# The end of a mixture-of-experts layer: last weight copy on GpSimd, late matmuls inside both branches, merges behind the late loads

## What is computed

```python
# xn: RMS-normalised x, 1024 x 1024; 64 experts of width 256, top 8 per token, plus one shared expert
def swiglu(x, w_gate, w_up, w_down):
    return (silu(x @ w_gate) * (x @ w_up)) @ w_down
routed = sum over the 8 experts e of a token: weight[token, e] * swiglu(xn[token], w_eg[e], w_eu[e], w_ed[e])
out = x1 + routed + swiglu(xn, w_sg, w_su, w_sd)        # x1: x after the output projection
```

## Time and profile before

| | us |
|---|---|
| median of 3 runs | 1374.88 (1374.83 to 1376.29) |
| profiled execution, its own time | 1375.44 |
| span of that execution, first to last instruction | 1373.7 |
| last job's down product starts and ends on PE | 1331.67, 1335.33 |
| six loads and three merges issued from | 1341.84 and 1342.37 |
| last add on DVE ends | 1371.32 |

### The profile page before, as it was taken

The page is one execution under the profiler, slowest core; times in us unless marked ns, Lnnn a source line. Parts: engine busy times, 40 slices in busy tenths (PEclk is TensorE's granted clock), DMA queues, the critical chain, the costliest instruction groups (busy, mean ns, idle before and its releaser), DMA issues.

```text
span 1373.7 us, 23742 instructions
## 1 busy us (share of the span) xinstructions
PE 1346.1 (98%) x5711; PEld 552.6 (40%) x5712; DVE 991.1 (72%) x2364; ACT 695.3 (51%) x654; POOL 563.2 (41%) x713
## 2 busy tenths in 40 slices
PE   7999999999999989999999999999999999999998
PEld 3445455555555433333333333333333333333333
DVE  2656655656544468888888888888888888888852
ACT  1223334243244214666666666666666666666640
POOL 3010313313121553555555555555555555555531
PEclk9999999999999999999999999999999999999999
DMA  9522212112029437999999999889999999999927
GB/s 341 213 76 85 62 54 85 57 59 85 6 80 397 140 132 291 347 317 365 305 364 375 332 311 358 275 267 290 333 328 378 368 345 319 333 333 303 355 38 217
DMA packets 77039, 333.74 MB, mean 243 GB/s; under 512 B 16119, under 2 KB 17656, under 8 KB 51332
## 3 DMA queue, kind: packets, MB, share of 16 engines
q1 hardware_dynamic: 46148, 253.29, 47.5%
q0 software_dynamic: 30848, 79.94, 23.5%
HBM read 286.41 MB, written 65.11 MB: 256 GB/s over the span
## 4 chain that ended last, share of the span: by engine, by line
PE 92%; DMA 2%; SPq 1%; issue 1%; POOL 1%; DVE 1%; ACT 0%; ACTq 0%; POOLq 0%; DVEq 0%
PE psP L766 57%; PE psW L766 32%; DMA u_dram<-eq 1%; PE psW L815 1%; SPq L410 1%; PE psT L846 1%; PE psT L862 1%; POOL slot_table L647 0%; SPq L403 0%; DMA area<-xn_dram,rows_i 0%; DMA area<-in_x_dram 0%; PE psW L835 0%; SPq L406 0%; DVE bias L1725 0%; DMA tabT<-slot_table,jobrow_i 0%
## 5 line engine op out<-in xcount | busy, mean ns | idle before, releaser
L766 PE MATMUL psP<-wts,bias 128*64 (+1 forms) x1296 | 571.8, 594 | 3.8 <-DVE bias L1725 3.8
L766 PE MATMUL psP<-area,bias 128*64 128x512 f32 x1264 | 557.1, 594 | 0.0
L766 PE MATMUL psW<-wts,area 128*64 (+2 forms) x1592 | 427.5, 593 | 1.4 <-ACT wts L1306 0.9
L1725 DVE STREAM_TRANSPOSE bias<-area 64x512 f32<-64x512 f32 x316 | 352.2, 1115 | 7.0 <-DMA area<-xn_dram,rows_i 1.4
L766 PEld LDWEIGHTS psP<-wts,bias 128*64 128x64 f32 (+1 forms) x1296 | 179.2, 139 | 366.3 <-issue 366.2
L1746 DVE STREAM_TRANSPOSE area<-dsq 32x64 f32<-32x64 f32 x1264 | 298.4, 236 | 22.4
L766 PE MATMUL psP<-wts,area 128*128 128x512 f32 (+1 forms) x704 | 291.2, 563 | 7.5 <-DMA wts<-in_w_in_dram 5.0
L1313 ACT ACTIVATE area<-wts 128x4096 f32 x77 | 278.6, 3618 | 13.7 <-issue 5.8
L766 PEld LDWEIGHTS psW<-wts,area 128*64 128x64 f32 (+1 forms) x1592 | 152.8, 147 | 247.9 <-issue 245.3
L1296 ACT ACTIVATE area<-psW 128x1024 f32<-128x1024 f32 x79 | 80.9, 1024 | 232.1 <-PE psW L766 160.7
L697 POOL DMA_INDIRECT area<-xn_dram,gidx x150 | 155.9, 1039 | 93.0 <-POOL gidx L693 65.4
(11 more groups left out here) (234 smaller groups left out, 748.9 us busy)
## 6 DMA issues: line engine op xcount, KB each, us to landing
wts<-in_w_exp_gate_dram SPq DMA_DIRECT2D x64, 1024.0 KB, 9.3
wts<-in_w_exp_up_dram SPq DMA_DIRECT2D x64, 1024.0 KB, 12.8
wts<-in_w_exp_down_dram SPq DMA_DIRECT2D x64, 1024.0 KB, 7.3
wts<-in_w_in_dram SPq DMA_DIRECT2D x4, 2048.0 KB, 17.6
area<-in_x_dram SPq DMA_DIRECT2D x15, 512.0 KB, 3.7
wts<-in_w_out_dram SPq DMA_DIRECT2D x1, 4096.0 KB, 18.4
area<-u_dram SPq DMA_DIRECT2D x16, 256.0 KB, 2.9
xn_dram<-area POOLq DMA_DIRECT2D x16, 256.0 KB, 2.8
```

The lines of the kernel that those rows point to most:

```text
L766: return nc.tensor.matmul(out_, lhsT, rhs, start=start, stop=stop)
L1725: i = V.transpose(xT[par][u * HB:(u + 1) * HB, :, b * HB:(b + 1) * HB] .rearrange("p k (g t) -> p g k t", g=2), rows[:, u])
```

## The change

Three edits:

1. The last job's `copy_dn` goes from ACT to POOL: a new function `copy_dn_last`, called in POOL's `last_jobs` between the scatters of the second and the third of the last four jobs. It waits for the same things as ACT's copy did. ACT keeps the copy of the job before.
2. On PE the rest of the late tiles moves into `end_of_jobs`, so that it stands in each of the two blocks; the load of n behind the blocks is gone.
3. POOL waits for all six loads of the late tiles (`ab_ld`) before it issues the merges.

```diff
@@ POOL @@
+            def copy_dn_last(n_less_2):
+                r = n_less_2 + 1
+                x = pool.value_load(ringB_i[0:1, bass.ds(r, 1)], min_val=1, max_val=NE)
+                pool.wait_ge(s_down, r + NSH)
+                for sl in range(NSLOT):
+                    loads = (x + (NSLOT - sl)) // NSLOT
+                    pool.wait_ge(dn_ld[sl], (loads + (1 >> loads)) * 16)
+                nc.gpsimd.tensor_copy(dn_b, wts[:, bass.ds((x % NSLOT) * SLOTW + 2 * GUW, FT * D)]).then_inc(s_dn_copy, 1)
+
             def last_jobs(par):
                 for m in range(4):
+                    if m == 2:
+                        copy_dn_last(n_less_4 + 2)
                     scatter(n_less_4 + (NSH + m), (par + m) % 2, n_less_4 * 3 + (2 * m))
...
             carry(pool)
+            for t in range(NLATE):
+                pool.wait_ge(ab_ld[t], 32)
             for a in range(MERGES):
@@ PE @@
                 gate_up_late(n, 0, range(0, 3))
                 down_halves(n + (NSH - 1), (par + 1) % 2, (last % NSLOT) * SLOTW)
+                gate_up_late(n, 0, range(3, KT))
+                for t in range(1, NLATE):
+                    gate_up_late(n, t, range(0, 2))
+                    t_h_late(n + NSH, t - 1)
+                    gate_up_late(n, t, range(2, KT))
+                    down_late(n + NSH, t - 1)
+                t_h_late(n + NSH, NLATE - 1)
+                down_late(n + NSH, NLATE - 1)
 
             with pe.If_ne(one, 0):
                 end_of_jobs(1)
             with pe.If_eq(one, 0):
                 end_of_jobs(0)
-            n = pe.value_load(n_jobs[0:1, 0:1], min_val=MIN_JOBS, max_val=JMAX)
-            gate_up_late(n, 0, range(3, KT))
-            for t in range(1, NLATE):
-                gate_up_late(n, t, range(0, 2))
-                t_h_late(n + NSH, t - 1)
-                gate_up_late(n, t, range(2, KT))
-                down_late(n + NSH, t - 1)
-            t_h_late(n + NSH, NLATE - 1)
-            down_late(n + NSH, NLATE - 1)
@@ ACT @@
-                    copy_dn(n_less_4 + (2 + m), e)
+                    if m == 0:
+                        copy_dn(n_less_4 + 2, e)
```

## The result

The changed kernel takes 1378.34 us, median of 10 runs (1376.74 to 1381.15), beside 1374.86 us (10 runs, 1373.91 to 1376.63) for the kernel before. The ratio is 1.0023, with a 95% interval of 1.0014 to 1.0032: slower by 3.5 us, where 3.3 us less were forecast.

The account below looks back on a forecast made before the run. PE's stall and clock fall were taken to bound the end: -2.19 - 1.96 + 0.2 = -3.95 us. Merges behind the loads, ending at 1370.3, limited the gain to 3.3: median 1371.6, 8-in-10 range 1370.3 to 1374.6.

Parts of the forecast that it names:

- first path: PE, DVE and the last stores in sequence at the kernel's end; forecast 3.95 us shorter, ending at 1369.75.
- the restart: Slow start of PE's late matmuls after a stop; the other 0.26 of 1.96 us expected to go.
- the stall: PE's 2.19 us "issue" wait at the branch and load of n before the late matmuls; forecast to go.
- the fall of the clock: PE at 1.2 GHz for a while after its idle time; 1.70 us of clock missing, forecast to go.
- second path: SP waiting for POOL's merges at the kernel's end; forecast to come later, ending at 1370.3.
- completion and end: Last term of the merges' path, from the end of their transfer to the span's end; taken as 0.65 us.
- Some tenths more: At the kernel's end, the last halves' stores meet the merges' tail; this brings the span to 1370.4.
- 3.89 us of idle time: POOL's idle time before the last job's scatter; said to cover its scatters' 2.8 us delay, with 0.6 coming through.
- (a): Rival: merges at the end bind in earnest; gain only 0.4 to 2.7 us, median 1372.2 to 1374.5; chance 0.24.
- (c): Rival: slower than before, the POOL copy taking over 5.6 us; median 1377.8 and more; chance 0.05.
- (b): Rival: the weight copy is slow on POOL, 3.1 to 4.6 us; median 1372.5 to 1375.0; chance 0.12.
- (d): Rival: PE still waits for code in the longer block, stall and clock fall stay; median 1375.1; chance 0.07.

Follow-up runs that it names:

- k8: k1 with the second half of the last late tile's store issued by POOL instead of SP; +5.66 us, ratio 1.0042 against the kernel before.
- k6: The changed kernel with the third merge alone, 2.1 of 2.62 MB left out; -2.22 us, ratio 0.9983 against the kernel before.
- k1: The kernel before with only the late matmuls moved inside PE's blocks; -0.92 us, ratio 0.9991 against the kernel before.
- k5: The changed kernel with the last down weight copy back on ACT; +1.21 us, ratio 1.0007 against the kernel before.
- k3: The kernel before with only the merges' wait for the six loads added; +1.31 us, ratio 1.0009 against the kernel before.
- k4: The changed kernel without the merges' wait for the six loads; +1.28 us, ratio 1.0009 against the kernel before.
- b3: The kernel before, unchanged, executed and profiled once more; that execution took 1375.94 us.
- k2: The kernel before with only the last down weight copy moved to POOL; +0.72 us, ratio 1.0002 against the kernel before.

## Why the prediction was wrong

**The first path: right up to the last add.** It was put at -3.95 us; the last add went from J + 43.33 to J + 39.32, 4.01 less. That the two are so close is in part luck: the copy was to lose 0.2 us and gained 0.05, and the 14 matmuls were to lose 1.96 us and lost 1.76, as 0.2 of the time put down to the restart stayed with no stop ahead of it. The copy on POOL took 1.89 us (2.2 taken, 1.85 to 4.6 the bounds), the last job's product starts at J + 3.63 where it started at J + 3.68, the stall and the fall of the clock are gone, and the branch at PE's end costs nothing. The copy took 1.89 us for 2048 elements per partition; the lower of the two figures of the GPSIMD Engine Reference of the Trainium skill (Performance versus the Vector engine), 1.03 cycles per element, gives an estimated 1.8 and agrees, 2.6 cycles does not.

**The second path: this step failed.** The sum was J + 42.3 us for its end, and it came at 46.42. Term by term, from the rows above:

| term | taken | measured |
|---|---|---|
| first load after J | 14.46 | 15.33 |
| loads, first issue to last landing | 9.2 | 9.8 |
| merges issued after that | 0.8 | 0.6 |
| first merge data after the issue | 2.6 | 1.65 |
| merges' transfer with the stores beside it | 14.6 | 15.3 |
| completion and end | 0.65 | 3.8 |

The last term carries 3.1 of the 4.1 us. It was taken from the way a store ends, for which SP waits by a semaphore. POOL has one more wait, its own DRAIN, and the prediction has no term for it. The row was there in the trace of before, where it ended at J + 38.5, seven microseconds before SP's and 3.5 us after the last merge data. One smaller reading was off, too: a scatter's data were said to follow in about 1.4 us; where the scatter waited for no landing they came 2.0 us after its start, in before. k8, in which nothing but a last store moves to POOL, shows that the DRAIN closes the kernel when POOL's data come late; k6, in which they come early, shows that it then does not.

**The stores beside the merges: a second miss, hidden behind the first.** "Some tenths more" was the price for the meeting of the last stores and the merges' tail. SP's DRAIN ends at J + 45.0 in after, 5.7 us after the last add; in k1 and in before it is 2.6 and 2.1. So without POOL's DRAIN the tail would still have been 45.2 us, not 42.4. Over 1362 to 1366 us q0 had 104 packets at 110.1% of 16 engines, 0.68 us each, and q1 had none with a 512 KB store waiting. It was no single event: stores issued while merges ran alone had no packet for 3.8 us in k5 and 4.2 and 3.1 us in k3, and landed after 7.8, 11.4 and 5.7. The sum had shared out engine time as if both queues got what they asked for. The Trainium skill's page "DMA: Bandwidth & Descriptors" (Queues, rings and completion order) says that each engine takes turns between queues only at whole packets of several descriptors; that is in line with a store held back for microseconds, but the runs here don't show the turns themselves.

**The scatters: 0.6 us taken, 1.5 measured,** outside of 0.2 to 1.3. The 3.89 us of idle time were named as cover. They weren't free: the scatter ahead lands in them. With POOL's scatters of the job before the last 2.5 us later (1333.20, J + 4.6, against J + 2.1), the last job's scatter into `out2` starts 5.6 us after the one ahead of it, and that into `x1_dram` 6.4 us after; both are ended by the landing. Beside edit 2 the price of edit 1 came to 2.2 us at the median (k4 less k1); in the profiled executions late tile 2's loads landed 3.6 us later there.

**The base.** 3.3 us were taken from one profiled execution and carried over to the median. 1.70 of them were the fall of the clock, which two more executions of before don't have. From the tail of those two, 43.75 us, the first path could gain 2.1 us at the last add, not 4. The time of the profiled execution, 0.56 us *above* the median, could not tell: b3, without a fall, took 0.75 us more than the median of the kernel before beside it, as J came late. With the tail of 43.75 the sum is: 43.75 to 46.42 us, +2.7, beside the +3.48 at the median. The rest is within what executions of the changed kernel differ by (its profiled run, at 1376.74 us, was its fastest).

**The rivals.** (a) had the right place, merges that bind in earnest, but ended at "no difference", as it let the completion at 0.65. (c), the rival on the slow side, needed a slow copy, and the copy was fast. (b) and (d) fell. The slow side came by a mechanism that none of them had.

**What stays open.** Why POOL's DRAIN needs 3.3 to 4.3 us behind the last data (k8's store: 3.4 us to its landing, 7.9 us to the end of the DRAIN). Why a store issued while merges run gets its first packet so late. Why k4's last loads took 2 us longer than k2's. And how the fall of the clock is spread over many executions of before: two more were looked at.

## What to carry over

Before moving a transfer towards the end of a kernel, look at the last instruction of each engine's stream: the end is the latest of these, and POOL, having issued transfers, closed 3.3 to 4.3 us after their last data here, so that what comes last should be issued by an engine that closes sooner. Idle time in front of an instruction is cover only if no landing runs inside it. And a stall's side effects, such as a fall of the clock, should be seen in a second execution of the kernel before before they go into the sum as a gain.

## What the runs showed that was not expected

- POOL's DRAIN at the end of its stream ended 3.3 to 4.3 us after the last data of its accumulating transfers, in 13 of 13 executions with such an end, whether 0.52 or 2.62 MB went ahead; behind a plain store issued by POOL, 7.9 us after the issue (k8). SP's took 13 ns.
- Accumulating transfers of 8 KB a packet, at 0.68 us each, kept a 512 KB store on the other queue without a packet for 3.7 us; the store landed after 9.2 us, where late tile 1's store took 2.6 us in before, behind the merges.
- A branch between PE's two blocks took 3.55 to 4.95 us in six executions, and at PE's end 7.2 us in after, but 3.5 us in k6 with most of the merges left out. It ended 2.3 to 2.6 us after the start of a 16 KB instruction packet each time, and that packet came 1.0 us after the branch's start in k6 and 4.75 us after it in after. A load of a register behind it took 0.6 to 0.7 us more.
- A copy of 128 x 2048 float32 from SBUF to SBUF on POOL took 1.89 us, no longer than ACT's 1.92.
